# Gate GEMMs of a two-layer recurrence: another spacing, and gates kept on chip

## The chip, the cores and the metric

The kernel runs on one core of one Trainium2 chip. The metric is the device time of one execution in microseconds. The core has five engines that run their own instruction streams and meet at semaphores: TensorE (PE, matmuls into PSUM), VectorE (DVE), ScalarE (ACT), GpSimd (POOL) and SyncE (SP, which here only issues the weight loads).

## The reference

The reference is a two-layer block followed by a second block of one layer, on 16 + 512 tokens of width 1024. What matters here is the mixing part of each of the two layers:

```
c_q, c_kv, k_pe, hq, hf, hi, hg, ga, gb = split_cols(u @ w_in[l], IN_SPLITS)
y_a = mla(...) @ w_proj_attn[l]
y_b = hgrn2(hq, hf, hi, hg, lbs[l], hg_norm[l]) @ w_proj_rec[l]
merged = jax.nn.sigmoid(ga) * y_a + jax.nn.sigmoid(gb) * y_b
h = h + merged @ w_out[l]
```

ga and gb are the gates, 2 x 1024 columns of u @ w_in. hgrn2 is a gated linear recurrence with 4 heads of 128 x 128 state: inside a chunk each output row is a decayed sum over earlier rows, and a state is carried between chunks. Its output is normalised per head, multiplied by silu(hg) and projected.

## The kernel before

Activations lie transposed: 128 channels on the partitions, the tokens along the free dimension (528 in layer 0, the 512 real ones in layer 1's gates and projections). A GEMM unit is one 128-column block of a weight. To keep float32 accuracy each operand is split into a high and a low part, and a unit is three terms (L571 to L576, matmuls at L573 and L575). For each unit SP loads raw weights into one of four slots (L405), ACT makes the high part `wh` (`hi`, L973) and POOL the low part `wl` (`split`, L474). ACT does that for unit k + 3 in `ahead(l, k)`, so the place of that call in ACT's order sets when POOL's split runs. A unit's result goes to one of two PSUM pairs; TensorE may start unit k when VectorE has evacuated unit k - 2 (L562). `evac` (L1396 to L1399) is that evacuation, with a multiplication by `rstd` or by a gate.

The recurrence of a layer goes over five tiles of tokens, of 16 rows and 4 x 128 rows. A tile of 128 rows has 8 levels m = 0 to 7 (the 16-row tile has 5), so there are 37 levels, numbered `lv` = 0 to 36. Level m adds the pairs of rows whose distance falls in blocks of 2^m. For each level VectorE prepares operands `qd` and `kd` (L1704, L1705), updates the running products `suf` and `HF` (L1711, L1713), and merges the result of the level before under a mask (`merge`, L1682 and L1686). TensorE runs four small matmuls per level (L789, shown as x8), may not start level lv before `kd_ready` of it, nor before `merged_lv` of level lv - 2. VectorE's semaphore steps follow one another in order. Behind a tile's last level come `kh` and `qt` (L1717, L1718), four transposes (L801), the output matmuls (L805, L808), the state matmuls (L813) and VectorE's state update (L1723, L1726).

Between the levels TensorE runs the 16 gate GEMMs of the layer (units U_GATE + g, L791 and L792): one behind level 0, and one behind each odd level from 3 to 31. VectorE evacuates a gate into one of two staging buffers `gst` two levels later (`due`, L1660, and `gate`, L1465); ACT applies the sigmoid, stores the gate to `gate_scratch` in memory and runs `ahead` (`gate`, L1051). At the last tile ACT issues the load of all 16 gates to `gat` (`gates_back`, L1063), whose place is that of the activations xh and xl, free by then.

Behind the recurrence (L817 to L836) TensorE sums the squares of two heads (`hg_sum`, L822), then runs the eight projections of the attention branch, two for each head, with the sums of heads 2 and 3 between them, and then the eight of the recurrent branch. Beside it VectorE takes for each head a reciprocal (L1736) and two products (L1737, L1738), waits for `gates_in` once, evacuates two projections with their gates (L1742) and makes a low part (L1744). `merged` (L1477 on VectorE, L1070 on ACT) joins the two branches.

The order on each engine is written out by hand; there is no planner in this part. Parts of the second block use the same gate store and load.

## Time and profile before

| | us |
|---|---|
| median of 3 runs | 3425.16 |
| lowest and highest | 3420.05, 3425.9 |
| the profiled execution | 3419.99 |
| its span, first to last instruction | 3418.1 |
| recurrence of layer 0, first level to last state matmuls | about 672 to 824 |
| recurrence of layer 1 | about 1952 to 2099 |

The profile is of one execution. A row of a timeline gives the start from the span's start, the duration, engine, source line, operation, what it writes and reads, how many such instructions stand together, and in brackets the idle time of the engine just before and who ended it. A matmul in float32 appears as two instructions. PEclk is TensorE's granted clock as a share of the full one; its two levels are 1.2 and 2.4 GHz.

### The profile page before, as it was taken

What the parts mean: (1) busy time and instruction counts of PE and PEld (TensorE: products, weight loads), DVE (VectorE), ACT (ScalarE), POOL (GpSimd) and SP (SyncE); (2) the same over time, 40 slices, a digit from 0 to 9 for tenths busy, and PEclk for the clock granted to TensorE, in tenths of its full rate; (3) what the DMA queues carried; (4) which work ended last, traced back from release to release, by engine and by line L of the source; (5) the groups of instructions that cost most, each with busy time, mean ns of one, the idle gap of its engine ahead of it and who ended that gap; (6) DMA issues with size and microseconds to landing.
All of it is one profiled execution on the core that took longest, in us unless ns stands there. A gap on an engine that the chain in (4) does not pass through costs nothing.

```text
span 3418.1 us, 54419 instructions
## 1 busy us (share of the span) xinstructions
PE 3280.1 (96%) x21472; PEld 2961.2 (87%) x21472; DVE 1392.2 (41%) x2138; ACT 1053.0 (31%) x1485; POOL 1278.9 (37%) x589
## 2 busy tenths in 40 slices
PE   8999989999999999999989998999997988999999
PEld 8999988898999999999989887788775676778887
DVE  4121443477521123121353487522336766552212
ACT  4222433322332224222343322332233433242222
POOL 3444432122444434434432122444436351144443
PEclk9999999999999999999999999999999988999999
DMA  4333321133332323333322133333232432233333
GB/s 131 92 88 91 89 62 50 47 92 106 99 93 87 92 86 93 92 92 89 90 64 62 41 93 111 114 92 96 88 87 65 96 77 91 74 100 98 93 93 98
DMA packets 544842, 298.63 MB, mean 87 GB/s; under 512 B 23281, under 2 KB 528625, under 8 KB 544561
## 3 DMA queue, kind: packets, MB, share of 16 engines
q1 hardware_dynamic: 514128, 258.77, 26.6%
q10 hardware_dynamic: 30560, 37.72, 3.4%
q8 instruction: 108, 1.77, 0.2%
q14 instruction: 46, 0.37, 0.0%
HBM read 278.36 MB, written 16.91 MB: 86 GB/s over the span
## 4 chain that ended last, share of the span: by engine, by line
PE 66%; issue 23%; POOL 6%; DVE 4%; ACT 1%; ACTq 0%; DMA 0%; POOLq 0%; DVEq 0%; SPq 0%
PE pair L575 37%; PE pair L573 27%; POOL wl L474 5%; DVE xl L1413 0%; PE aux L599 0%; DVE negt L1888 0%; DVE tmp L1412 0%; PE aux L930 0%; DVE top L1887 0%; PE aux L931 0%; PE pair L877 0%; ACT xh L987 0%; DVE tmp L1860 0%; PE aux L655 0%; ACT tmp L986 0%
## 5 line engine op out<-in xcount | busy, mean ns | idle before, releaser
L474 POOL TENSOR_TENSOR wl<-raw,wh 128x1024 fp32r<-128x1024 f32 (+4 forms) x549 | 1222.6, 2229 | 2098.8 <-ACT wh L973 2098.3
L973 ACT ACTIVATE wh<-raw 128x1024 fp32r<-128x1024 f32 (+4 forms) x549 | 528.1, 964 | 475.6 <-DMA raw<-ffn_w_down 160.5
L1399 DVE TENSOR_TENSOR tmp<-pair,rstd 128x528 f32<-128x528 f32 (+1 forms) x222 | 155.7, 702 | 812.5 <-PE pair L575 500.1
L575 PE MATMUL pair<-xh,wh 128*128 128x264 f32 x3072 | 462.1, 290 | 17.3 <-DVE xl L1413 12.2
L575 PE MATMUL pair<-xh,wl 128*128 128x264 f32 x3072 | 447.0, 285 | 0.9 <-POOL wl L474 0.9
L575 PE MATMUL pair<-xl,wh 128*128 128x264 f32 x3072 | 447.3, 285 | 0.0
L575 PEld LDWEIGHTS pair<-xh,wh 128*128 128x128 f32 x3072 | 404.4, 190 | 25.3 <-ACT wh L973 9.3
L575 PEld LDWEIGHTS pair<-xh,wl 128*128 128x128 f32 x3072 | 403.4, 189 | 1.2 <-POOL wl L474 1.2
L575 PEld LDWEIGHTS pair<-xl,wh 128*128 128x128 f32 x3072 | 403.9, 189 | 0.0
L1423 DVE SCALAR_TENSOR_TENSOR hT<-pair,hT 128x528 f32 (+3 forms) x144 | 100.7, 700 | 474.0 <-PE pair L575 273.0
L573 PE MATMUL pair<-xh,wh 128*128 128x512 f32 x1064 | 289.5, 405 | 3.7 <-issue 2.2
L573 PE MATMUL pair<-xh,wl 128*128 128x512 f32 x1064 | 282.8, 399 | 5.7 <-POOL wl L474 5.7
L573 PE MATMUL pair<-xl,wh 128*128 128x512 f32 x1064 | 280.1, 396 | 0.0
L573 PEld LDWEIGHTS pair<-xh,wl 128*128 128x128 f32 x1064 | 202.7, 191 | 54.0 <-POOL wl L474 6.5
L573 PEld LDWEIGHTS pair<-xh,wh 128*128 128x128 f32 x1064 | 200.2, 191 | 53.9 <-issue 8.3
L573 PEld LDWEIGHTS pair<-xl,wh 128*128 128x128 f32 x1064 | 201.0, 189 | 45.4
L1013 ACT ACTIVATE ah<-tmp 128x528 f32 (+3 forms) x110 | 70.4, 640 | 533.1 <-DVE tmp L1448 533.1
L575 PE MATMUL pair<-ah,wh 128*128 128x264 f32 x1320 | 203.9, 287 | 13.6 <-DVE R L1630 6.0
L575 PE MATMUL pair<-al,wh 128*128 128x264 f32 x1320 | 201.0, 285 | 0.0
L575 PE MATMUL pair<-ah,wl 128*128 128x264 f32 x1320 | 200.6, 285 | 0.0
L575 PEld LDWEIGHTS pair<-ah,wh 128*128 128x128 f32 x1320 | 177.9, 189 | 16.1 <-issue 11.3
L1010 ACT ACTIVATE tmp<-tmp 128x528 f32<-128x528 f32 (+1 forms) x110 | 70.4, 640 | 353.3 <-DVE tmp L1399 353.3
(320 smaller groups left out, 3973.6 us busy)
## 6 DMA issues: line engine op xcount, KB each, us to landing
raw<-ffn_w_gu SPq DMA_DIRECT2D x176, 512.0 KB, 3.8
raw<-w_in SPq DMA_DIRECT2D x103, 512.0 KB, 3.9
raw<-ffn_w_down SPq DMA_DIRECT2D x64, 512.0 KB, 3.8
raw<-ffn_w_down SPq DMA_DIRECT2D x32, 384.0 KB, 3.3
raw<-w_out SPq DMA_DIRECT2D x24, 512.0 KB, 3.8
raw<-w_ffn_gate SPq DMA_DIRECT2D x22, 512.0 KB, 3.7
raw<-w_ffn_up SPq DMA_DIRECT2D x22, 512.0 KB, 3.8
gate_scratch<-gst ACTq DMA_DIRECT2D x32, 256.0 KB, 2.3
```

The source lines that it names most:

```text
L474: nc.gpsimd.tensor_tensor(wl[:, k % SPL, 0:n], raw[:, k % SPL, 0:n], wh[:, k % SPL, 0:n].bitcast(F32), ALU.subtract).then_inc(S["split_don ...
L573: return nc.tensor.matmul(pp[:, 0, :], wk, x[:, kk, t0:t0 + SEQ], start=first, stop=last)
L575: mm = nc.tensor.matmul(pp[:, h, 0:th], wk, x[:, kk, t0 + h * th:t0 + (h + 1) * th], start=first, stop=last)
L973: nc.scalar.activation(wh[:, k % SPL, 0:n], raw[:, k % SPL, 0:n], ACT.Copy).then_inc(S["split_hi"], 1)
L1010: nc.scalar.activation(tm(SG, T), tm(GS, T), ACT.Silu).then_inc(S["silu_done"], 1)
L1013: nc.scalar.activation(ah[:, bass.ds(j + i * 2, 1), 0:T].rearrange("p o t -> p (o t)"), tm(A32, T), ACT.Copy).then_inc(S["ahi_done"], 1)
L1399: v.tensor_tensor(halves(dst, th), psum_pair(0 if alone else k, th), halves(scale, th), ALU.mult).then_inc(S["evacuated"], 1)
L1423: v.scalar_tensor_tensor(halves(hm, T // 2), psum_pair(k, T // 2), factor, halves(hm, T // 2), ALU.mult, ALU.add).then_inc(S["evacuated"], 1)
```

## The change

Gate GEMMs 0 to 13 stand behind the levels of a list, GATE_AT, which are two or three levels apart: in each tile of 128 rows behind its levels 0, 3 and 6. GEMM 14 stands behind the last tile's state matmuls, GEMM 15 behind the sums of squares of the first two heads. VectorE evacuates gates 0 to 12 two levels later as before, gate 13 ahead of the last tile's last merge, gate 14 ahead of the first head, gate 15 behind the first head's products. ACT's `ahead` calls move along; the sigmoids of gates 14 and 15 come behind the four heads. Each gate of the layers has a place of its own in SBUF (`homes`), so their store and load go. The second block keeps its store and load, with its own functions. The diff, cut to the layers' part:

```diff
@@ -288,7 +288,8 @@
         relb = [ybuf, z_out]
         negq = [negr[:, 64 * i * (i + 1):64 * (i + 1) * (i + 2)] for i in range(4)]
         negm = [negt[:, 64 * i * (i + 1):64 * (i + 1) * (i + 2)] for i in range(4)]
-        gates1 = gat[:, :].rearrange("p (m t) -> p m t", t=T1)
+        homes = [R[:, 4608 + i * T1:4608 + (i + 1) * T1] for i in range(12)] + [negt[:, 0:T1], negt[:, T1:2 * T1], gst[:, 0, :], gst[:, 1, :]]
+        GATE_AT = (0, 3, 5, 8, 11, 13, 16, 19, 21, 24, 27, 29, 32, 35)
         gates2 = gat[:, 0:2 * KD * SEQ].rearrange("p (m t) -> p m t", t=SEQ)
         hgv = [gst[:, 0, :], gst[:, 1, :], negt[:, 0:T1], negt[:, T1:2 * T1]]
...
@@ -788,8 +789,8 @@
                                 lt, rt, n = kd[m % 2][:, h, 0:sz], qd[m % 2][:, h, 0:sz // 2], sz // 2
                             mm = nc.tensor.matmul(bank[lv % 2][0:sz, h * 128:h * 128 + n], lt, rt, start=True, stop=True)
                         mm.then_inc(S["lv_done"], 1)
-                        if lv == 0 or lv >= 3 and lv % 2 == 1 and lv // 2 < 2 * KD:
-                            gemm(l, U_GATE + lv // 2, KD, (xh, xl), T // 2, t0=t0)
+                        if lv in GATE_AT:
+                            gemm(l, U_GATE + GATE_AT.index(lv), KD, (xh, xl), T // 2, t0=t0)
                         lv += 1
                     if i == 0:
                         pe.wait_ge(S["vt_copied"], l * 10 + 10)
...
@@ -822,9 +823,11 @@
                         mm = nc.tensor.matmul((aux45, aux67)[h % 2][:, x, 0:th], ones, tm(HSQ[h % 2])[:, x * th:(x + 1) * th],
                                               start=True, stop=True)
                     mm.then_inc(S["hgss"], 1)
+                gemm(l, U_GATE + 2 * KD - 2, KD, (xh, xl), T // 2, t0=t0)
                 pe.wait_ge(S["s_ready"], l * 5 + 5)
                 hg_sum(0)
                 hg_sum(1)
+                gemm(l, U_GATE + 2 * KD - 1, KD, (xh, xl), T // 2, t0=t0)
                 for h in range(HG):
                     for x in range(2):
                         gemm(l, U_PROJ + 2 * h + x, 4, (ah[:, 0:4, :], al[:, 0:4, :]), T // 2, t0=t0,
...
@@ -1048,24 +1051,18 @@
                     act.wait_ge(S["evacuated"], U(l, ub + m) + 1 + PAIRS)
                     act.dma_start(out[m * P:(m + 1) * P, :], hT[:, m, N_META:T1]).then_inc(S["stored"], 16)
-            def gate(l, ub, g, T, sets):
-
-                act.wait_ge(S["evacuated"], U(l, ub + g) + 1 + PAIRS)
-                if l is None:
-                    ins = nc.scalar.activation(gst[:, g % 2, 0:T], gst[:, g % 2, 0:T], ACT.Tanh, scale=0.5)
-                else:
-                    ins = nc.scalar.activation(gst[:, g % 2, 0:T], gst[:, g % 2, 0:T], ACT.Sigmoid)
-                ins.then_inc(S["gate_sig"], 1)
-                act.wait_ge(S["gate_sig"], sets * (2 * KD) + g + 1)
-                act.dma_start(gscr[g, :, 0:T], gst[:, g % 2, 0:T]).then_inc(gate_stored[g % 2], 16)
-                ahead(l, ub + g)
-
-            def gates_back(l, ub, T, dst, sets):
-
-                for x in range(2):
-                    act.wait_ge(gate_stored[x], sets * (KD * 16) + KD * 16)
-                act.wait_ge(S["gemm_done"], U(l, ub + 2 * KD) + SPL)
-                act.dma_start(dst, gscr[:, :, 0:T].rearrange("m p t -> p m t")).then_inc(S["gates_in"], 16)
+            def gate(l, g, T):
+
+                act.wait_ge(S["evacuated"], U(l, U_GATE + g) + 1 + PAIRS)
+                nc.scalar.activation(homes[g][:, 0:T], homes[g][:, 0:T], ACT.Sigmoid).then_inc(S["gate_sig"], 1)
+
+            def gate2(g):
+
+                act.wait_ge(S["evacuated"], U(None, U_GATE2 + g) + 1 + PAIRS)
+                nc.scalar.activation(gst[:, g % 2, 0:SEQ], gst[:, g % 2, 0:SEQ], ACT.Tanh, scale=0.5).then_inc(S["gate_sig"], 1)
+                act.wait_ge(S["gate_sig"], DEPTH * (2 * KD) + g + 1)
+                act.dma_start(gscr[g, :, :], gst[:, g % 2, 0:SEQ]).then_inc(gate_stored[g % 2], 16)
+                ahead(None, U_GATE2 + g)
             def merged(l, ub, T, m0):
...
@@ -1162,12 +1159,10 @@
                 lv = g = 0
                 for i, (st, sz) in enumerate(TT1):
                     lv += sz.bit_length()
-                    while g < 2 * KD and 2 * g + 3 < lv:
-                        gate(l, U_GATE, g, T, l)
+                    while g < len(GATE_AT) and (GATE_AT[g] + 2 < lv or i == len(TT1) - 1):
+                        gate(l, g, T)
+                        ahead(l, U_GATE + g)
                         g += 1
-                    if i == len(TT1) - 1:
-                        assert g == 2 * KD
-                        gates_back(l, U_GATE, T, gates2 if T == SEQ else gates1, l)
                     act.wait_ge(S["kht_done"], l * 5 + i + 1)
                     nc.scalar.activation(khT[0:sz, :, :], bank[3][0:sz, :].rearrange("p (h k) -> p h k", h=HG),
                                          ACT.Copy).then_inc(S["kht_copied"], 1)
...
@@ -1189,8 +1184,10 @@
                 hg_square(1)
                 for j in range(4):
                     nc.scalar.activation(ah[:, j, t0:T1], oT[:, j, t0:T1], ACT.Copy).then_inc(S["oth"], 1)
+                ahead(l, U_GATE + 2 * KD - 2)
                 hg_rms(0)
                 hg_rms(1)
+                ahead(l, U_GATE + 2 * KD - 1)
                 for h in range(HG):
                     act.wait_ge(S["yb_in"], l * HG + h + 1)
                     nc.scalar.activation(ah[:, 4 + h, :], tm(A32), ACT.Copy).then_inc(S["ybhi"], 1)
...
@@ -1200,6 +1197,8 @@
                         ahead(l, U_PROJ + 2 * h + x)
                     if h < HG - 2:
                         hg_rms(h + 2)
+                for g in (2 * KD - 2, 2 * KD - 1):
+                    gate(l, g, T)
                 merged(l, U_PROJ + KD, T, l * KD)
                 residual(l, U_WO, nb + 3, lambda m: gcur[:, 2 * KD + m:2 * KD + m + 1], T)
                 if l < DEPTH - 1:
...
@@ -1485,11 +1472,12 @@
                         dve.wait_ge(S["m_ready"], m0 + m - 1)
                     buf = tm(MB[m % 2], T)
                     if l is None:
-                        evac_tanh(ub + m, buf, gates[:, KD + m, :])
+                        evac_tanh(ub + m, buf, gates[KD + m])
                     else:
-                        evac(l, ub + m, buf, gates[:, KD + m, :], T // 2)
+                        dve.wait_ge(S["gate_sig"], l * (2 * KD) + KD + m + 1)
+                        evac(l, ub + m, buf, gates[KD + m], T // 2)
                     dve.wait_ge(S["evacuated"], U(l, ub + m) + 1 + PAIRS)
-                    v.tensor_tensor(buf, buf, gates[:, m, :], ALU.add).then_inc(S["m_done"], 1)
+                    v.tensor_tensor(buf, buf, gates[m], ALU.add).then_inc(S["m_done"], 1)
                     if m >= 1:
                         lo(m - 1)
                 lo(KD - 1)
...
@@ -1655,12 +1643,15 @@
                 attention(at1[l], oT, hg_inputs, lambda n: hg_evac(n, 0))
                 t0, T = real(l)
-                gates = gates2 if T == SEQ else gates1
+                gates = [x[:, 0:T] for x in homes]
+
+                def gate(g):
+                    evac(l, U_GATE + g, gates[g], rstd[:, t0:T1], T // 2)
                 def due(lv):
-                    if lv >= 3 and lv % 2 == 1 and lv // 2 - 1 < 2 * KD:
-                        gate(l, U_GATE, lv // 2 - 1, T, l, rstd[:, t0:T1])
+                    if lv - 2 in GATE_AT:
+                        gate(GATE_AT.index(lv - 2))
                 lv = 0
                 for i, (st, sz) in enumerate(TT1):
...
@@ -1716,6 +1707,9 @@
                         lv += 1
                     v.tensor_tensor(kh[:, :, 0:sz], HK[:, :, st:st + sz], suf[:, :, 0:sz], ALU.mult)
                     v.tensor_tensor(qt[:, :, 0:sz], HQ[:, :, st:st + sz], HF[:, :, st:st + sz], ALU.mult).then_inc(S["kq_ready"], 1)
+                    if i == len(TT1) - 1:
+                        assert GATE_AT[-1] == lv - 2
+                        gate(len(GATE_AT) - 1)
                     merge(nl - 1, lv - 1)
                     dve.wait_ge(S["ds_done"], l * 5 + i + 1)
                     ds = bank[3].rearrange("p (h v) -> p h v", h=HG)
...
@@ -1730,6 +1724,7 @@
                 for j in range(4):
                     dve.wait_ge(S["oth"], l * 4 + j + 1)
                     v.tensor_tensor(al[:, j, t0:T1], oT[:, j, t0:T1], ah[:, j, t0:T1].bitcast(F32), ALU.subtract).then_inc(S["yo_ready"], 1)
+                gate(2 * KD - 2)
                 for h in range(HG):
                     dve.wait_ge(S["hgrms"], l * HG + h + 1)
                     g = tm(HRMS[h % 2])
...
@@ -1737,9 +1732,10 @@
                     step(v.tensor_tensor(tm(US), HQ[:, h, :], g, ALU.mult))
                     v.scalar_tensor_tensor(tm(A32), tm(US), pcur[:, 13:14], HGT[:, h, :], ALU.mult, ALU.mult).then_inc(S["yb_in"], 1)
                     if h == 0:
-                        dve.wait_ge(S["gates_in"], l * 16 + 16)
+                        gate(2 * KD - 1)
+                        dve.wait_ge(S["gate_sig"], l * (2 * KD) + KD)
                     for x in range(2):
-                        gated(l, U_PROJ + 2 * h + x, 2 * h + x, gates, T)
+                        evac(l, U_PROJ + 2 * h + x, gates[2 * h + x], gates[2 * h + x], T // 2)
                     dve.wait_ge(S["ybhi"], l * HG + h + 1)
                     v.tensor_tensor(al[:, 4 + h, :], tm(A32), ah[:, 4 + h, :].bitcast(F32), ALU.subtract).then_inc(S["yo_ready"], 1)
                 merged(l, U_PROJ + KD, gates, T, l * KD)
```

## Rows read from the trace of the kernel before

**Rows 1.** the page: span, and part 1, busy time and share of each engine
```profile
span 3418.1 us, 54419 instructions
...
PE 3280.1 (96%) x21472; PEld 2961.2 (87%) x21472; DVE 1392.2 (41%) x2138; ACT 1053.0 (31%) x1485; POOL 1278.9 (37%) x589
```

**Rows 2.** windows: stretch; its us, PE, PEld, DVE, ACT, POOL busy, PEclk, DMA share, GB/s
```profile
689.00:809.00 120.00, 118.73 (x986) 117.74 (x985) 97.97 (x165) 27.25 (x35) 32.28 (x14) 0.99 0.29 84
...
809.00:827.00 18.00, 12.94 (x64) 11.79 (x64) 11.48 (x27) 5.07 (x9) 1.43 (x1) 0.72 0.73 269
...
1968.00:2084.00 116.00, 114.27 (x649) 98.25 (x649) 97.69 (x165) 26.80 (x35) 32.45 (x14) 1.00 0.29 86
...
2084.00:2102.00 18.00, 12.59 (x64) 11.56 (x64) 11.04 (x26) 4.67 (x9) 1.41 (x1) 0.72 0.74 264
```

**Rows 3.** timeline of PE, layer 0: start us, us, engine, line, operation [idle before <-releaser]
```profile
759.35 2.18 PE L575 MATMUL pair<-xh,wh 128*128 128x264 f32 x16
...
765.24 1.00 PE L789 MATMUL aux<-tmp 128*128 128x64 f32 x8
...
766.55 1.10 PE L789 MATMUL aux<-tmp 128*128 128x64 f32 x8 [0.31 <-DVE tmp L1705]
```

**Rows 4.** timeline of DVE, one tile of layer 0, then two state updates of layer 1
```profile
758.74 1.12 DVE L1726 SCALAR_TENSOR_TENSOR R<-R,HF,aux 128x128 f32<-128x128 f32 x4 [3.04 <-PE aux L813]
...
774.12 0.71 DVE L1399 TENSOR_TENSOR gst<-pair,rstd 128x528 f32<-128x528 f32 x1
...
776.92 0.42 DVE L1711 TENSOR_TENSOR tmp<-tmp,HF 128x256 f32<-128x256 f32 x1
...
777.38 2.50 DVE L1713 TENSOR_TENSOR HF<-HF 128x256 f32<-128x256 f32 x1
...
789.70 0.44 DVE L1686 COPY_PREDICATED R<-con,aux 128x256 f32<-128x256 int32 x1 [0.91 <-PE aux L789]
...
793.18 1.12 DVE L1726 SCALAR_TENSOR_TENSOR R<-R,HF,aux 128x128 f32<-128x128 f32 x4 [3.04 <-PE aux L813]
...
2035.16 1.12 DVE L1726 SCALAR_TENSOR_TENSOR R<-R,HF,aux 128x128 f32<-128x128 f32 x4 [3.04 <-PE aux L813]
...
2069.05 1.12 DVE L1726 SCALAR_TENSOR_TENSOR R<-R,HF,aux 128x128 f32<-128x128 f32 x4 [3.04 <-PE aux L813]
```

**Rows 5.** timeline of POOL, the same tile of layer 0
```profile
777.04 2.55 POOL L474 TENSOR_TENSOR wl<-raw,wh 128x1024 fp32r<-128x1024 f32 x1 [5.19 <-ACT wh L973]
```

**Rows 6.** timeline of PE, end of the recurrence of layer 0
```profile
811.82 1.97 PE L789 MATMUL aux<-tmp 128*128 128x64 f32 x8 [2.66 <-DVE tmp L1705]
...
824.87 2.05 PE L822 MATMUL aux<-tmp,con 128*128 128x264 f32 x8 [1.22 <-DVE R L1726]
...
834.87 1.54 PE L575 MATMUL pair<-ah,wh 128*128 128x264 f32 x8 [2.13 <-DVE gat L1399]
...
839.41 1.05 PE L822 MATMUL aux<-tmp,con 128*128 128x264 f32 x4
```

**Rows 7.** timeline of PE, end of the recurrence of layer 1
```profile
2085.73 1.10 PE L789 MATMUL aux<-tmp 128*128 128x64 f32 x8 [1.21 <-DVE tmp L1705]
...
2088.86 1.97 PE L789 MATMUL aux<-tmp 128*128 128x64 f32 x8 [2.02 <-DVE tmp L1705]
...
2100.55 2.05 PE L822 MATMUL aux<-tmp,con 128*128 128x264 f32 x8 [1.22 <-DVE R L1726]
...
2110.49 1.16 PE L573 MATMUL pair<-ah,wh 128*128 128x512 f32 x4 [2.31 <-DVE gat L1399]
```

**Rows 8.** timeline of DVE, first heads of layer 0 behind the recurrence
```profile
829.11 3.45 DVE L1736 RECIPROCAL tmp<-tmp 128x528 f32<-128x528 f32 x1 [0.98 <-ACT tmp L1183]
...
835.88 3.45 DVE L1736 RECIPROCAL tmp<-tmp 128x528 f32<-128x528 f32 x1
```

**Rows 9.** timeline of ACT, first merged tile of layer 0
```profile
861.82 0.65 ACT L1074 ACTIVATE mh<-tmp 128x528 fp32r<-128x528 f32 x1 [3.71 <-DVE tmp L1492]
```

**Rows 10.** DMA issues by line: out<-in engine, count, KB each, us to landing
```profile
gat<-gate_scratch ACTq DMA_DIRECT2D x2, 4096.0 KB, 14.6
```

More of the change, by code:

```diff
@@ L1233, in gates @@
                 for g in range(g0, g1):
-                    gate(None, U_GATE2, g, SEQ, DEPTH)
+                    gate2(g)
             def square2(j):
@@ L1463, in ffn @@
                     f0 += nf
-            def gate(l, ub, g, T, sets, scale):
-                if g >= 2:
-                    dve.wait_ge(gate_stored[g % 2], sets * (KD * 16) + g // 2 * 16)
-                evac(l, ub + g, gst[:, g % 2, 0:T], scale, T // 2)
-            def gated(l, k, m, gates, T):
-                if l is None:
-                    return evac_tanh(k, gates[:, m, :], gates[:, m, :])
-                evac(l, k, gates[:, m, :], gates[:, m, :], T // 2)
             def merged(l, ub, gates, T, m0):
@@ L1866, in gates @@
                 for g in range(g0, g1):
-                    gate(None, U_GATE2, g, SEQ, DEPTH, rstd2[:, :])
+                    if g >= 2:
+                        dve.wait_ge(gate_stored[g % 2], g // 2 * 16)
+                    evac(None, U_GATE2 + g, gst[:, g % 2, 0:SEQ], rstd2[:, :], th)
             def index_score(n):
@@ L1972, in more2 @@
                         if k == U_PROJ2:
-                            dve.wait_ge(S["gates_in"], DEPTH * 16 + 16)
-                        gated(None, k, k - U_PROJ2, gates2, SEQ)
+                            dve.wait_ge(S["gates_in"], 16)
+                        evac_tanh(k, gates2[:, k - U_PROJ2, :], gates2[:, k - U_PROJ2, :])
             def s5_out(n):
@@ L2005, in _ @@
                 v.tensor_tensor(al[:, j, 0:SEQ], oT[:, j, 0:SEQ], ah[:, j, 0:SEQ].bitcast(F32), ALU.subtract).then_inc(S["yo_ready"], 1)
-            merged(None, U_PROJ2 + KD, gates2, SEQ, DEPTH * KD)
+            merged(None, U_PROJ2 + KD, [gates2[:, m, :] for m in range(2 * KD)], SEQ, DEPTH * KD)
             residual(None, U_WO2, 0.5, X2, n2 + 1, lambda m: vec[:, V_GAIN + 64 + m:V_GAIN + 65 + m], SEQ)
```

6 lines of the change are left out of this document (3 added, 3 removed).

## Prediction, made before the change was run

> **What bounds the kernel now.** The page comes first: TensorE is busy for 96% of the span, VectorE for 41% [rows 1]. Over the whole kernel TensorE is the bound, and whatever is only moved from one place on TensorE to another keeps its price. The change touches the recurrence of two layers, so the stages are read next. In the long stretch of the recurrence, before the last levels, TensorE is busy for 118.73 of 120 us, but VectorE for 97.97 of them as well; in the 18 us after it TensorE is busy for 12.94 us only, at a granted clock of 0.72; layer 1 shows the same, 114.27 of 116 us and then a clock of 0.72 [rows 2]. So there are two places with different limits. In the tail (levels 32 to 36, the last state update, the first projections) TensorE waits and runs at the lower of its two clock levels for part of the time: this is what the change fills. In the body TensorE looks full, and the question is how much room VectorE has once GEMMs are taken out of it.
>
> The timeline answers that. TensorE in the body runs a gate GEMM of 5.89 us (759.35 to 765.24), then a level, waits 0.31 us, and runs a second level ahead of the next GEMM [rows 3]. VectorE's state updates stand 34.44 us apart in layer 0 (758.74 to 793.18) and 33.89 us in layer 1 (2035.16 to 2069.05) [rows 4]. Inside that tile VectorE is idle for only two stretches of note: 0.91 us for the last level, and 3.04 us for the matmuls of output and state, which no placement of gate GEMMs removes [rows 4]. The rest is a chain of small steps, one of which takes 2.50 us where the one ahead of it took 0.42 us: it starts 0.34 us after a GpSimd split that lasts 2.55 us (777.04) and ends 0.29 us after it [rows 4, 5]. Each gate GEMM brings one such split with it, so each costs VectorE about 2.08 us beside the evacuation of 0.71 us, some 0.1 of which overlaps the next step and leaves 0.62 [rows 4]. The Trainium skill, "SBUF — State Buffer", section "SBUF: two separate sides", says that VectorE with two SBUF inputs and GpSimd share a port pair under an exclusive lock held for a whole instruction; by that rule the split delays VectorE wherever in the tile it falls. The row agrees with 2.08 us.
>
> **The change part by part.**
>
> *Body.* A full tile (8 levels) now has three gate GEMMs, behind its levels 0, 3 and 6, where it had four. TensorE's work falls from 34.44 to 34.44 - 5.89 = 28.6 us. VectorE's falls by one evacuation, one lock and the idle 0.91 us: 34.44 - 0.62 - 2.08 - 0.91 = 30.8 us. So VectorE's chain becomes the bound of the tile, and TensorE waits about 2 to 3 us in it, in two wide gaps: it has two levels to run behind a GEMM and must wait for the third, whose operands VectorE can only finish after the evacuation and two rounds of steps. These waits run in a ring, since VectorE must in turn wait for the end of a GEMM that started late: stepping through a tile with the spacings of [rows 3, 4], VectorE comes to the evacuation of the second gate at 17.0 us, and that GEMM ends at 17.5 us. I add 0.6 us: 31.4 us. The bounds are 30.8 (no wait) and 33.5 us (a lock of 2.08 us falls ahead of the third level and passes through TensorE in full). The last tile took 30.5 us before (793.14 to 824.87 - 1.22) [rows 4, 6] with its last gates' splits of half size; it now has three GEMMs with full ones, so it is like the others. The 16-row tile loses about 1 us, as its gate is evacuated a level sooner. Layer 0: before 3 x 34.44 + 30.5 = 133.8, after 4 x 31.4 + 1 = 126.6, a gain of 7.2 us. Layer 1: before 3 x 33.89 + 30.3 (2069.05 to 2100.55 - 1.22) = 132.0 [rows 4, 7], after, with the same sum from 33.89, 4 x 31.1 + 1 = 125.4, a gain of 6.6 us.
>
> *The stage behind the last state update.* Before, the first reciprocal of VectorE starts at 829.11 and the second at 835.88, that is 5.5 and 12.2 us after the last state matmuls (823.65), and each later head takes 6.77 us again [rows 6, 8]. A head's TensorE work (two projections of 2.9 us, half of a gate GEMM, and a sum of 0.8 us) is as long, 6.7 us. So this stage has no room either: both engines are full in it. Now TensorE runs gate GEMM 14 (5.9), the two sums (1.7), GEMM 15 (5.9), projection 0 (2.9) and projection 1 (2.9) in a row, and the second head's reciprocal stands on VectorE's queue behind the evacuation of projection 1: 19.3 us plus 1.4 for handing over, that evacuation and one step, some 20.7 us instead of 12.2. Cost 8.5 us in layer 0 and, with 512 columns for 528, 8.2 in layer 1. What waits behind the moved evacuations is ScalarE's next square and the third sum. The two sigmoids of ScalarE come after the heads, where it was idle for 3.71 us before the first merged tile [rows 9]: nothing; without that cover two sigmoids and a table change, some 2.6 us.
>
> *Memory.* The stores of the layers' 32 gates and their two loads of 4 MB (14.6 us to landing) [rows 10] go. In the long stretches the 16 DMA engines were 0.29 busy [rows 2], and no idle time of TensorE ended on a DMA in the rows of the tail [rows 6, 7]: nothing, at most 0.4 us per gate on ScalarE, which is not on the path.
>
> *Sum without the clock:* layer 0 -7.2 + 8.5 = +1.3, layer 1 -6.6 + 8.2 = +1.6, together +3 us. The tail's waits of 2.66, 1.21, 2.02, 1.22, 2.13 and 2.31 us [rows 6, 7] are really filled; they come back as waits in the wide gaps.
>
> *The clock.* Where TensorE had only short levels and a wait between them, it fell: behind the 2.66 us wait the levels take 1.97 us each instead of 1.10 [rows 3, 6], in layer 1 the same after waits of 1.21 and 2.02 us [rows 7]. Behind a wait of 2.13 us the projection takes 4.54 us instead of 2.9 (834.87 to 839.41), and behind 2.31 us in layer 1 the first third takes 1.16 us, so there it did not fall [rows 6, 7]. That is three of four, and a short fall costs 1.6 to 1.8 us. Each layer now has eight wide gaps, each with three short levels and a wait of 1.1 to 2.7 us between two GEMMs. I let 5 or 6 of 8 fall: 5.5 x 1.75 = 9.6 us a layer, 19 us in all, and they count in full, since VectorE waits for the slowed GEMM. Bounds: 0 (none) and 28 us (all).
>
> By the Trainium skill, "TensorE: Matmul & The Clock Gate", section "Why this matters for your kernels", only long idle gaps between bursts make the clock drop, and gaps like these would not. The rows show drops at shorter waits. By that rule the sum stays at +3 us; it is the first rival.
>
> Sum: +3 + 19 = +22 us on the profiled execution of 3419.99 us (span 3418.1 [rows 1] and 1.9 around it), 3442 us. The median of the runs stands 5.2 us above that execution: 3447 us.
>
> **The rivals.**
>
> *A, the clock holds.* The wide gaps are broken by too short waits, and a GEMM stands close on both sides. For it: after 2.31 us it held once. Against: three of four fell, with the same short levels. Time: 3425.2 + 3 = 3428, with the tile bounds 3423 to 3440.
>
> *B, faster.* The tail's gain stays and the body doesn't pay. Mechanism: a lock costs VectorE nothing if it falls into one of its own waits, above all the 3.04 us before the state update; ScalarE no longer spends 0.4 us on issuing the store, so each split starts sooner, and gaps between splits are wider. If one of the three locks of a tile falls into a wait, a tile takes 31.4 - 2.1 = 29.3 us; over eight tiles 17 us, and the clock then holds as the third level comes earlier: 3425.2 + 3 - 17 = 3411 us. It decides from about one hidden lock in every second tile on. Against it: a split follows the evacuation of its gate by 2.9 us (774.12 to 777.04) [rows 4, 5], and no evacuation stands that far ahead of the state matmuls.
>
> *C, the ring is worse.* Locks ahead of the third level in half of the tiles (another 8 us) and nearly all gaps fall (9 us more): 3464 us.
>
> **How the numbers follow.** Forecast (slower by 9 to 33 us) 0.53; A 0.22; B 0.13; C 0.12. Some 0.2%, 7 us, is what a measurement of this kernel can tell from no change. Faster by more: B, and the low end of A, 0.14. Within: most of A, 0.20. Slower: the forecast, C and the top of A, 0.66. The range leaves out B's better half and the upper end of C: 3417 to 3464.
>
> **What would show it.** Right: state updates 31 to 33 us apart; TensorE waiting 1 to 3 us for VectorE behind two levels in tiles 1 to 4; a granted clock of 0.85 to 0.95 in the body where it was 0.99; no wait over 1 us between level 35 and projection 0; the second reciprocal some 20 us behind the last state matmuls. Wrong: tiles under 30.5 us, or a body at full clock (rival A), or locks in the wait for the state matmuls (B). The weakest term is the number of falls.

## The result and the profile after

The changed kernel takes 3488.86 us in the median (3483.77 to 3492.14), the kernel before 3425.53 us beside it. The ratio is 1.0182, with a 95% interval of 1.016 to 1.0205: it is slower by 63 us, where 22 were forecast, and above the range of 3417 to 3464. The sign was right and the size was not: a lock that the prediction had put at nothing fell on the critical operand, and the clock fell more often and at a higher price than it had taken.

The page of the changed kernel, its span and the busy time and share of each engine, to be held against [rows 1]:

```profile
span 3484.0 us, 54385 instructions
...
PE 3319.3 (95%) x21472; PEld 2994.0 (86%) x21472; DVE 1388.7 (40%) x2138; ACT 1054.8 (30%) x1489; POOL 1276.9 (37%) x589
```

TensorE is busy for 39 us more, though it does the same 21472 instructions: they took longer. VectorE and GpSimd are unchanged. The windows say where (columns as in [rows 2]; the first is the same stretch of layer 0 as there, the second the tail, which now ends some 15 us later, the third the whole run of the four 128-row tiles of layer 1):

```profile
689.00:809.00 120.00, 104.02 (x769) 102.36 (x769) 80.34 (x147) 19.93 (x28) 23.40 (x10) 0.89 0.18 45
824.00:842.00 18.00, 16.57 (x141) 16.20 (x140) 12.39 (x24) 6.73 (x12) 3.85 (x2) 1.00 0.10 30
1997.00:2146.00 149.00, 127.65 (x660) 109.65 (x658) 101.10 (x182) 24.76 (x34) 31.02 (x13) 0.87 0.16 41
```

The body, which had 118.73 us of TensorE work in 120 us at a clock of 0.99 [rows 2], now has 104.02 at 0.89. The tail rose from 12.94 us at 0.72 to 16.57 at 1.00, so the waits and the low clock of the tail did go in layer 0; in layer 1 the same 18 us (2131 to 2149) have 16.59 us at 0.91, where they had 12.59 at 0.72. The tiles of layer 1 ran at 0.87 on average.

From here on a tile is counted from the end of the state matmuls of one tile to the end of those of the next. Before, the four tiles of 128 rows took 35.7, 34.5, 34.4 and 30.5 us in layer 0 and 33.4, 33.8, 33.9 and 30.3 us in layer 1: 135.1 and 131.5 us. After, they take 35.1, 38.5, 39.5 and 35.4, and 35.9, 37.8, 37.7 and 37.6: 148.5 and 149.0 us. The 16-row tile ahead of them, counted from its first level, went from 16.7 to 17.7 and from 15.9 to 16.8 us. Here is one such tile of layer 1, TensorE first:

```profile
2077.24 2.11 PE L790 MATMUL aux<-tmp 128*128 128x64 f32 x16
2083.39 1.97 PE L790 MATMUL aux<-tmp 128*128 128x64 f32 x8 [4.04 <-DVE tmp L1696]
2085.12 3.76 PE L574 MATMUL pair<-xh,wh 128*128 128x512 f32 x8
2088.68 2.40 PE L574 MATMUL pair<-xl,wh 128*128 128x512 f32 x8
...
2095.85 1.56 PE L790 MATMUL aux<-tmp 128*128 128x64 f32 x8 [1.18 <-DVE tmp L1696]
2097.17 3.27 PE L574 MATMUL pair<-xh,wh 128*128 128x512 f32 x8
...
2107.56 1.06 PE L814 MATMUL aux<-R,tmp 128*128 128x128 f32 x8
```

There are two wide gaps. In the first TensorE waits for 4.04 us, and the level behind it takes 1.97 us and the first term of the GEMM 3.76 us, at the lower level of the clock; the whole GEMM takes 7.65 us (2085.12 to 2092.77) instead of 5.66 (2071.58 to 2077.24). In the second it waits for 1.18 us, and behind that the clock falls too: the level takes 1.56 us and the GEMM 6.83 us (2097.17 to 2104.00). VectorE and GpSimd in the same tile:

```profile
2080.41 0.45 DVE L1695 TENSOR_TENSOR tmp<-HQ,HF 128x256 f32<-128x256 f32 x1
2080.78 2.56 DVE L1696 TENSOR_TENSOR tmp<-HK,tmp 128x256 f32<-128x256 f32 x1
2083.37 0.42 DVE L1702 TENSOR_TENSOR tmp<-tmp,HF 128x256 f32<-128x256 f32 x1
...
2093.04 0.69 DVE L1398 TENSOR_TENSOR R<-pair,rstd 128x512 f32<-128x512 f32 x1 [5.13 <-PE pair L574]
```

```profile
2080.61 2.45 POOL L475 TENSOR_TENSOR wl<-raw,wh 128x1024 fp32r<-128x1024 f32 x1 [3.04 <-ACT wh L976]
```

More than half of the 4.04 us comes from the second row. It is `kd` of the third level, the very operand that TensorE waits for: 2.56 us instead of 0.41, that is 2.15 us more, under the split that GpSimd had started 0.17 us earlier. It is so in all eight full tiles of the two layers. The last row shows the ring from the other side: VectorE waits for 5.13 us for the GEMM that started late and ran slowly.

The stage behind the last state matmuls of layer 0, on VectorE (state update, first and second reciprocal), to be held against [rows 8]:

```profile
839.04 1.12 DVE L1720 SCALAR_TENSOR_TENSOR R<-R,HF,aux 128x128 f32<-128x128 f32 x4 [3.04 <-PE aux L814]
...
846.47 3.45 DVE L1731 RECIPROCAL tmp<-tmp 128x528 f32<-128x528 f32 x1 [0.92 <-ACT tmp L1178]
...
859.48 3.45 DVE L1731 RECIPROCAL tmp<-tmp 128x528 f32<-128x528 f32 x1
```

The state matmuls end at 838.99, so the first two reciprocals stand at 7.5 and 20.5 us, where they stood at 5.5 and 12.2 us. The third and fourth follow at 27.2 and 35.3 us, for 21.0 and 27.7 before.

### The profile page after: what moved, and what is told of

Same layout as the page of the kernel before. It is cut to its first block, busy times and chain, and to the rows that moved or that the text cites. A ratio compares the mean times of both kernels' runs of the same rounds, so it can differ in the third digit from the quotient of the medians.

```text
span 3484.0 us, 54385 instructions
## 1 busy us (share of the span) xinstructions
PE 3319.3 (95%) x21472; PEld 2994.0 (86%) x21472; DVE 1388.7 (40%) x2138; ACT 1054.8 (30%) x1489; POOL 1276.9 (37%) x589
## 4 chain that ended last, share of the span: by engine, by line
PE 64%; issue 24%; POOL 6%; DVE 4%; ACT 1%; DMA 1%; ACTq 0%; POOLq 0%; DVEq 0%; SPq 0%
PE pair L576 36%; PE pair L574 26%; POOL wl L475 5%; DVE xl L1412 0%; PE aux L600 0%; DVE negt L1886 0%; PE aux L933 0%; DVE top L1885 0%; PE aux L934 0%; DVE tmp L1411 0%; DMA raw<-ffn_w_gu 0%; PE pair L880 0%; DVE tmp L1856 0%; PE aux L656 0%; DVE tmp L1833 0%
## 5 line engine op out<-in xcount | busy, mean ns | idle before, releaser
L576 PE MATMUL pair<-xh,wh 128*128 128x264 f32 x3072 | 470.1, 293 | 18.8 <-DVE xl L1412 13.6
L576 PEld LDWEIGHTS pair<-xh,wh 128*128 128x128 f32 x3072 | 412.2, 193 | 26.7 <-ACT wh L976 9.3
L574 PE MATMUL pair<-xh,wh 128*128 128x512 f32 x1064 | 300.2, 417 | 1.5 <-DVE xl L1412 1.5
L574 PEld LDWEIGHTS pair<-xh,wh 128*128 128x128 f32 x1064 | 208.2, 198 | 53.9 <-issue 5.8
L576 PEld LDWEIGHTS pair<-al,wh 128*128 128x128 f32 x1320 | 178.7, 191 | 0.0
```

Source lines behind the costliest of these rows:

```text
L574: return nc.tensor.matmul(pp[:, 0, :], wk, x[:, kk, t0:t0 + SEQ], start=first, stop=last)
L576: mm = nc.tensor.matmul(pp[:, h, 0:th], wk, x[:, kk, t0 + h * th:t0 + (h + 1) * th], start=first, stop=last)
```

## The experiments

All tile times are read as above, and all ratios are to the kernel before on the same chip in the same sequence of runs. The kernel before took 3429.30 us there for the first four experiments, 3424.93 for the next four and 3426.57 for the last four.

### The gates on chip, with the old spacing

```diff
-        GATE_AT = (0, 3, 5, 8, 11, 13, 16, 19, 21, 24, 27, 29, 32, 35)
+        GATE_AT = (0, 3, 5, 7, 9, 11, 13, 15, 17, 19, 21, 23, 25, 27, 29, 31)
```

The two GEMMs, evacuations, `ahead` calls and sigmoids behind the recurrence go with it.

> The changed kernel with the gate GEMMs back where they stood before (behind level 0 and each odd level to 31, none behind the state matmuls), gates still kept on chip. Theory L+C (the time comes from the wider spacing, through the lock ahead of the third level and the clock that falls in the wide gaps): near the kernel before, 3425 us, perhaps 1 to 3 us under it as ScalarE no longer issues the stores. Rival M (the gates' new places on chip or the missing load cost the time): 3470 us or more, state updates over 36 us apart.

Measured: 3434.17 us, ratio 1.0017 (1.0005 to 1.0029). The tiles take 35.7, 34.0, 34.0 and 30.7 us in layer 0, and 33.1, 33.4, 33.4 and 29.5 in layer 1: 0.4 us less than before each in the middle ones. So keeping the gates on chip costs nothing in the stages that it touches; the median is dealt with at the end of this section. It does one thing that matters later. The same split of a middle tile in layer 1, first in the kernel before (VectorE's `kd` of the third level and the step behind it, then GpSimd), then in this one:

```profile
2045.49 0.41 DVE L1705 TENSOR_TENSOR tmp<-HK,tmp 128x256 f32<-128x256 f32 x1
2045.93 2.58 DVE L1711 TENSOR_TENSOR tmp<-tmp,HF 128x256 f32<-128x256 f32 x1
```

```profile
2045.82 2.41 POOL L474 TENSOR_TENSOR wl<-raw,wh 128x1024 fp32r<-128x1024 f32 x1 [3.55 <-ACT wh L973]
```

```profile
2045.47 2.62 DVE L1690 TENSOR_TENSOR tmp<-HK,tmp 128x256 f32<-128x256 f32 x1
```

```profile
2045.28 2.52 POOL L475 TENSOR_TENSOR wl<-raw,wh 128x1024 fp32r<-128x1024 f32 x1 [3.04 <-ACT wh L974]
```

Before, the split started 0.33 us after `kd` had, and held up the step behind it. Without the store that ScalarE used to issue between sigmoid and `ahead` it starts 0.52 us sooner against `kd`, 0.19 us ahead of it, and `kd` itself takes 2.62 us. At this spacing that is free, since a GEMM stands between the second and the third level. With the new spacing nothing does. There the split starts 2.38 us behind the evacuation of its gate (2078.23 to 2080.61), as in this kernel (2042.90 to 2045.28), where it was 2.90 us with the store (2042.92 to 2045.82). That the store at the new spacing would have kept `kd` free is worked out from these rows: no run has both.

### No lock: the low weight part of the gates written as zeros

```diff
+                nc.gpsimd.memset(wl[:, k % SPL, :].bitcast(F32), 0.0).then_inc(S["split_done"], 1)
```

in place of the split for gate GEMMs 3 to 15; everything else is the changed kernel.

> The changed kernel, but for gate units 3 to 15 GpSimd writes zeros to wl in place of the subtraction raw - wh, so the low part of these weights is left out of the result; the matmuls are the same. In the trace of the changed kernel a split of 2.45 us stood ahead of the third level's operands and stretched that step from 0.41 to 2.56 us. Theory L+C: if zeros hold VectorE up less than the subtraction, each full tile loses 2 us of lock in that gap and 2 to 2.5 us of falls with it, 37.7 us to 33 us, total about 3443 to 3450 us. Clock alone: the step is short but the clock falls all the same, 35.5 us a tile, 3470 us. Rival V (VectorE's own steps are too slow for three levels in a row, lock or not): no change, 3487 us. By the Trainium skill, SBUF - State Buffer, section SBUF: two separate sides, a two-input VectorE step is locked out only by a GpSimd operation that reads SBUF, so zeros should not hold it up at all.

Measured: 3449.35 us, ratio 1.0068 (1.0051 to 1.0084). The tiles take 36.1, 31.3, 31.2, 34.3 and 32.1, 30.4, 32.0, 33.5 us. GpSimd and TensorE in one tile of layer 1 and, for TensorE, the tile behind it:

```profile
2051.11 0.95 POOL L480 MEMSET wl<- 128x1024 f32 x1 [3.75 <-ACT wh L981]
```

```profile
2051.77 1.10 PE L795 MATMUL aux<-tmp 128*128 128x64 f32 x8 [1.40 <-DVE tmp L1701]
2052.69 2.10 PE L579 MATMUL pair<-xh,wh 128*128 128x512 f32 x8
...
2061.41 1.79 PE L795 MATMUL aux<-tmp 128*128 128x64 f32 x8 [1.18 <-DVE tmp L1701]
2062.96 3.05 PE L579 MATMUL pair<-xh,wh 128*128 128x512 f32 x8
...
2083.77 1.10 PE L795 MATMUL aux<-tmp 128*128 128x64 f32 x8 [1.40 <-DVE tmp L1701]
2084.68 3.06 PE L579 MATMUL pair<-xh,wh 128*128 128x512 f32 x8
```

Under these memsets, which read nothing, no step of VectorE in the tiles was held up. The first gap shrinks from 4.04 to 1.40 us; the rest of it is the evacuation and the steps between the GEMM's end and the third level. And the clock: behind a wait of 1.40 us the GEMM's first third ran at full speed in one tile (2.10 us) and at the lower level in the next (3.06 us), and behind 1.18 us it fell. Without locks the kernel is 40 us faster than the changed one, and falls remain in it (clock 0.94 and 0.95 over the four tiles of the layers).

### No falls, as far as fillers go: spare matmuls in the wide gaps

```diff
+        FILL = {7: 20, 10: 8, 15: 20, 18: 8, 23: 20, 26: 8, 31: 20, 34: 8}
...
+                        if lv in FILL:
+                            pe.wait_ge(S["o_evac"], l * 5 + i)
+                        for x in range(FILL.get(lv, 0)):
+                            nc.tensor.matmul(bank[2][:, 0:256], identr[:, :], xh[:, x % 8, 0:256], start=True, stop=True)
```

Added to the changed kernel.

> The changed kernel with extra matmuls of 256 columns into a free PSUM bank behind the second level of each wide gap of the full tiles, 20 in the first gap of a tile and 8 in the second (about 2.2 and 0.9 us, less than the waits of 4.04 and 1.18 us there). They compute nothing that is used. Theory L+C: the clock holds, each full tile goes from 37.7 to 33.3 us (the lock stays), total about 3447 us, granted clock in the body 0.98 or more. If the clock is not a cause but only goes along with the waits: no gain, 3487 us or more.

Measured: 3461.33 us, ratio 1.0102 (1.0083 to 1.012). In layer 0 the clock holds (1.00 over its four tiles) and they take 33.6, 33.9, 33.9 and 33.9 us, 13 us less than in the changed kernel, though TensorE does 112 matmuls more. In layer 1 the 20 fillers, 2.61 us in all, leave a wait of 1.66 us, and one fall stays in each of three tiles (clock 0.96; 34.4, 34.9, 34.9, 33.3 us). The tile was expected at 33.3, some 0.6 us too low, and the total at 3447, 14 us too low. The clock is a cause and not a companion: more work on TensorE made the kernel 28 us faster, 25 of them in the tiles. `kd` still takes 2.58 us here, so these tiles carry the lock without the falls: 33.9 us in layer 0.

### Neither lock nor falls

The zeros of the second experiment, and 8 fillers (1.19 us) in each wide gap.

> Both together: zeros in place of the splits of gate units 3 to 15 (their low weight part is left out of the result), and 8 extra matmuls behind the second level of each wide gap. Theory L+C: no lock and no fall, a full tile takes 30.5 to 31.4 us as I had predicted for the change without falls, total 3423 to 3430 us (what is gained in the body is paid behind it). If the two causes overlap: no better than the better of the two alone, about 3445 us.

Measured: 3438.51 us, ratio 1.0029 (1.0018 to 1.0041). The tiles take 33.0, 31.2, 31.2, 31.2 and 30.6, 30.4, 30.4, 30.4 us, at a clock of 0.99 and 1.00: the tile that was expected (the first of layer 0 apart), although the total is 8 to 15 us above what was. TensorE in one tile of layer 1, fillers and the levels behind them:

```profile
2047.38 1.19 PE L801 MATMUL aux<-xh,identr 128*128 128x256 f32 x8
2048.99 1.10 PE L796 MATMUL aux<-tmp 128*128 128x64 f32 x8 [0.41 <-DVE tmp L1706]
2049.90 2.07 PE L580 MATMUL pair<-xh,wh 128*128 128x512 f32 x8
...
2058.59 1.10 PE L796 MATMUL aux<-tmp 128*128 128x64 f32 x8 [0.18 <-DVE tmp L1706]
```

### Two GEMMs behind the last state update, with the old spacing ahead of them

```diff
-        GATE_AT = (0, 3, 5, 8, 11, 13, 16, 19, 21, 24, 27, 29, 32, 35)
+        GATE_AT = (0, 3, 5, 7, 9, 11, 13, 15, 17, 19, 21, 23, 25, 27)
```

> The first experiment's kernel (gates on chip, GEMMs behind level 0 and each odd level) up to gate GEMM 13 behind level 27; only GEMMs 14 and 15 move behind the last state matmuls, as in the changed kernel. It does the second part of the change alone. My sum for it: tiles 1 to 3 as in the first experiment (34.0 and 33.4 us), the last tile without any GEMM about 26 us instead of 30, the second reciprocal 20.5 us behind the last state matmuls instead of 12.2: +8.3 - 4.5 in each layer, 3434 + 8 = 3442 us, 3438 to 3446. Were the stage behind the recurrence the main cause of the change's loss, it would be at 3470 us or more.

Measured: 3441.05 us, ratio 1.0047 (1.003 to 1.0064), 6.9 us above the first experiment's median. The reciprocals stand at 7.5 and 20.5 us behind the state matmuls in layer 0 and at 7.2 and 19.7 in layer 1, exactly as in the changed kernel. The last tiles fall from 30.7 to 24.75 and from 29.5 to 25.9 us. Two GEMMs of 5.9 us left each of them and only 3.6 to 5.9 us came back: what is left of the tail is VectorE's chain and a clock that was low for much of it (0.65 and 0.60 over the last tiles). The stage costs 8 us a layer wherever the GEMMs came from.

### The same splits, started behind the third level's operand

```diff
+                    if g in (5, 8, 11, 14):
+                        pool.wait_ge(S["kd_ready"], l * LEVELS + GATE_AT[g - 3] + 4)
                     split(l, U_GATE + g, KD)
```

> The changed kernel, but GpSimd holds back one split in each tile of 128 rows (gate units 5, 8, 11, 14) until VectorE has made the third level's operands in the wide gap; nothing is left out. Theory L+C: the lock then falls beside the GEMM that follows, the third level starts 2.1 us sooner and fewer gaps fall: 33 to 34 us a tile instead of 37.7, total 3440 to 3452 us, near the kernel with zeros (3449). If it was not where the lock falls but that there is one: no gain, 3489 us.

Measured: 3456.23 us, ratio 1.0091 (1.0073 to 1.0109). No work is removed, four splits a layer start a little later, and the kernel is 33 us faster than the changed one by the medians, 28 us by the spans of the two profiles, 26.7 of them in the tiles. The tiles take 36.1, 31.7, 34.8, 33.2 and 32.1, 34.3, 34.3, 34.3 us; five of the eight are above the 33 to 34 us that were expected, and the total is 4 us above its range. TensorE in the last tile of layer 1:

```profile
2093.85 1.10 PE L793 MATMUL aux<-tmp 128*128 128x64 f32 x8 [1.89 <-DVE tmp L1699]
2094.76 3.08 PE L577 MATMUL pair<-xh,wh 128*128 128x512 f32 x8
...
2105.06 1.32 PE L793 MATMUL aux<-tmp 128*128 128x64 f32 x8 [1.18 <-DVE tmp L1699]
2106.14 3.50 PE L577 MATMUL pair<-xh,wh 128*128 128x512 f32 x8
```

The first wait is 1.89 us instead of 4.04, and in this tile the clock falls behind both: 3.08 and 3.50 us for a third of a GEMM that takes 2.1 us. In the tile of 31.7 us of layer 0 it fell behind neither.

### Both: splits behind the operand, and 8 fillers a gap

> The kernel that holds back the splits, with 8 extra matmuls of 256 columns behind the second level of each wide gap. Theory L+C: no fall and no lock on the ring, a tile takes 31.3 us in layer 0 and 30.7 in layer 1 as with zeros and extra matmuls, total 3430 to 3440 us, with the whole result computed.

Measured: 3441.96 us, ratio 1.005 (1.0032 to 1.0068), 2 us above what was expected, with every operation of the changed kernel in it. The tiles take 31.4, 31.7, 31.7, 31.7 and 30.7, 31.1, 31.1, 31.1 us at a clock of 1.00: the body that the prediction had drawn. The low weight parts are real ones here, so what the zeros gained was not due to the data. GpSimd's split, the step that it now holds up, and TensorE at that time:

```profile
2048.16 2.63 POOL L476 TENSOR_TENSOR wl<-raw,wh 128x1024 fp32r<-128x1024 f32 x1 [3.70 <-DVE tmp L1704]
```

```profile
2048.12 0.42 DVE L1710 TENSOR_TENSOR tmp<-tmp,HF 128x256 f32<-128x256 f32 x1
2048.58 2.50 DVE L1712 TENSOR_TENSOR HF<-HF 128x256 f32<-128x256 f32 x1
```

```profile
2048.14 1.10 PE L794 MATMUL aux<-tmp 128*128 128x64 f32 x8 [0.90 <-DVE tmp L1704]
...
2057.76 1.10 PE L794 MATMUL aux<-tmp 128*128 128x64 f32 x8 [0.18 <-DVE tmp L1704]
```

The lock of 2.08 us is still there, on the last step of the level (2.50 us for 0.42), and TensorE passes over it with a GEMM.

### Fillers in the tail of the kernel before

```diff
+        FILL = {33: 14, 34: 10, 35: 10}
```

Added to the kernel before, as 128-column matmuls.

> The kernel before with extra matmuls of 128 columns into a free PSUM bank behind levels 33, 34 and 35 (14, 10 and 10), where TensorE waited in the tail and its clock fell to 0.72 of full. If the clock holds, the last tile goes from 30.5 to about 29 us and the output and state matmuls run at full speed: 2 to 4 us less in each layer's tail, total 4 to 8 us under the kernel before. If the tail is VectorE's alone: no gain.

Measured: 3437.75 us, ratio 1.003 (1.001 to 1.0049): a miss. In layer 1 the clock held (1.00 over the four tiles) and the last tile fell from 30.3 to 28.1 us. In layer 0 it rose from 30.5 to 33.5 us:

```profile
807.78 1.76 PE L795 MATMUL aux<-identr 128*128 128x128 f32 x14
810.64 1.97 PE L790 MATMUL aux<-tmp 128*128 128x64 f32 x8 [1.10 <-DVE tmp L1710]
812.37 2.37 PE L795 MATMUL aux<-identr 128*128 128x128 f32 x10
```

Behind 14 fillers and a wait of 1.10 us the level takes 1.97 us, and now the fillers themselves are slow (10 in 2.37 us, where 14 took 1.76) and keep the next level waiting. Here a filler helped where the clock held; where it fell all the same, the filler was paid at the low level. The two tiles together are only 0.8 us longer than before, though the median is 12.8 us up: the rest is not in the stage that was edited (the last section of the experiments).

### Fillers in the tail with the gates on chip

```diff
+        FILL = {33: 8, 34: 6, 35: 6}
```

Added to the first experiment, as 256-column matmuls.

> The gates kept on chip with the old spacing, plus 8, 6 and 6 spare matmuls of 256 columns behind levels 33, 34 and 35 of each layer; their results are used nowhere. If the low clock of the tail is what costs there, the last tile takes 28 to 29 us in both layers (30.7 and 29.5 without them) and the kernel 1 to 4 us less than with the gates on chip alone, 3430 to 3433 us. If the fillers only move the fall of the clock, as in layer 0 of the kernel before with fillers, the last tile of layer 0 takes 33 us and the kernel 3435 to 3438 us.

Measured: 3433.64 us, ratio 1.0019 (1.0004 to 1.0033), and last tiles of 30.4 and 29.8 us for 30.7 and 29.5 without fillers. The clock over the four tiles rises from 0.95 and 0.96 to 0.97 and 0.97, and the fillers' own time takes it back. Neither theory's tile: nothing is won or lost, and no kernel tried here beats the kernel before.

### Three more profiles of the two kernels

The totals of several kernels stood some 10 us above what their tiles say. Their traces, and that of the changed kernel, have a stretch at the lower clock level in the attention of the second block, which the change doesn't touch, and which the first trace of the kernel before doesn't have. The kernel before and the changed one were profiled again, without any edit.

> The kernel before, unchanged, for one more profile. In the second block the trace of the changed kernel has one stretch of 20 to 24 us at the lower clock level, which costs some 10 us and which the first trace of before does not have. Theory S (it comes and goes from execution to execution, whatever the layers do): this profile or the third one of the kernel before shows it, and such an execution takes 3431 to 3438 us where those without it take 3423 to 3427. Theory V (the change brings it): no profile of the kernel before shows it.

> The kernel before, unchanged, once more, for the same question: S expects the low stretch in at least one of the two, at a time of 3431 to 3438 us; V expects none, and times of 3423 to 3427.

> The changed kernel, unchanged, for one more profile. Both theories: tiles of 37.6 to 38.5 us, 3484 to 3492 us. S: the low stretch of the second block can be absent here, and the time is then under 3485 us.

Measured: 3435.62, 3440.90 and 3487.38 us. The same stretch of the second block in the first profile of the kernel before, in the second, in the third, and in the changed kernel (columns as in [rows 2]):

```profile
2916.00:2936.00 20.00, 18.80 (x94) 12.92 (x95) 17.00 (x29) 6.71 (x19) 1.77 (x2) 1.00 0.05 14
```

```profile
2925.00:2945.00 20.00, 20.00 (x56) 13.19 (x56) 11.93 (x20) 4.27 (x12) 0.00 (x0) 0.51 0.00 1
```

```profile
2928.00:2952.00 24.00, 24.00 (x70) 15.82 (x69) 14.09 (x23) 5.00 (x14) 1.27 (x1) 0.51 0.00 1
```

```profile
2974.00:2997.00 23.00, 23.00 (x63) 14.93 (x63) 13.17 (x22) 4.72 (x12) 1.27 (x1) 0.50 0.00 1
```

With this stretch the kernel before ran at 0.51 for 20 to 24 us, and its place behind the stretch is 8 to 10 us later. It belongs to the execution, not to the change. The kernel before with fillers has it too, which is most of its 12.8 us. The 40 other executions of the kernel before in the three sequences lie between 3419.89 and 3437.72 us, 17 of them above 3430; every profile of a kernel with the change or a part of it has the stretch but for one (the zeros without fillers, 3437.63 us where its other executions took 3447.85 to 3452.06). Whether the change makes it more frequent, and by what, is open. Compared like with like, the second and third profiles of before (spans 3433.7 and 3439.0, mean 3436.3) and the two of after (3484.0 and 3485.2, mean 3484.6) lie 48.3 us apart. The other 15 of the 63 us fit this reading but aren't shown one by one: the first profile, from which the forecast counted, doesn't have the stretch, some half of the executions of before take as little time as it or little more, and both profiles of the changed kernel do have it. The second and third profiles of before are also 6 and 11 us behind the first already ahead of the stretch; by what is open. And of the 39 us that TensorE is busy longer in the changed kernel, 17 are there in these two profiles as well (3296.8 and 3297.1 us busy for 3280.1).

## Why the prediction was right in sign and wrong in size

The two layers against the prediction's terms, in us; the third column is read from the runs above.

| term | predicted | measured |
|---|---|---|
| body without locks ahead of the third level, without falls | -7.2 and -6.6 | -7.6 and -6.5 (tiles 126.5 and 124.1 of the kernel with later splits and fillers, for 135.1 and 131.5, and +1.0 and +0.9 in the 16-row tile of the first profile) |
| stage behind the last state update | +8.5 and +8.2 | +8.3 and +7.6 (second reciprocal 20.5 for 12.2, 19.7 for 12.1) |
| a lock ahead of the third level | 0 (a bound) | +8.6 and +8.6 (four tiles x 2.15, as 2.56 - 0.41) |
| falls of the clock | +9.6 and +9.6 | +13.4 and +16.3 (148.5 and 149.0, less 126.5 and 124.1 and less the lock) |
| memory traffic | 0 | 0 in the stages (first experiment) |
| sum | +22 | +48.7, for 48.3 between the profiles that are alike |

The falls can be counted in the changed kernel's own rows. From the start of a gap's third level to the next level behind the GEMM it is 6.8 us in layer 0 and 6.53 in layer 1 where the clock holds; it holds in 3 of the 16 wide gaps, and the other 13 are 1.6 to 3.1 us longer, 13.4 us in layer 0 and 15.0 of the 16.3 in layer 1. Of the 42 us between the forecast of 3447 us and the measured 3488.86, 17 are the lock, some 10 the falls, and some 15 what the last section of the experiments ascribes to the execution.

**The body.** The tile of 31.4 and 31.1 us was right to some 0.3 us (31.7 and 31.1 measured), for the kernel in which nothing locks the third level. Part of that is luck. The prediction took VectorE's chain as the bound and subtracted locks from it; but with all locks gone a tile still takes 31.2 and 30.4 us, only 0.5 and 0.7 less than with three of them, not 6 us less. What bounds it is the round trip in each wide gap: end of a GEMM, evacuation, two rounds of steps, `kd`, level, next GEMM, which leaves TensorE 1.2 to 1.4 us of wait a gap however free VectorE is elsewhere. The prediction did step through this ring, but added only 0.6 us for it to a chain with all its locks (30.8 us), and the chain with locks and the round trip without them happen to be about equally long. Three slips of its working were small: from 33.89 the same sum gives 30.9 us for layer 1 and not 31.1; the first tile of layer 0 took 35.7 us before and not 34.44; and rival A's upper bound, a tile of 33.5 us, gives 3445 us and not 3440.

**The lock, the step that failed.** The prediction named the mechanism and its price (2.08 us, passed through in full, a tile of 33.5 us) and put it at zero, or in rival C in half of the tiles. It fell on `kd` of the third level in every tile, since the order is the same in every tile. The rows to see it were there: the split of [rows 5] starts within a few tenths of a us of the steps it can hold, so 0.5 us decide which one. With the store gone it started 0.52 us sooner against `kd`, and by the rows of the first experiment that is the difference. The prediction mentioned those 0.4 us, but in rival B, as something that gives gaps between splits, and didn't ask onto which instruction the split would move. The experiment that delays four splits a layer is worth 26.7 us in the tiles, 17.2 of them the lock and the rest what the shorter wait does to the clock; the medians are 33 us apart, and the other 6 are not placed.

By the Trainium skill, "SBUF — State Buffer", section "SBUF: two separate sides", a VectorE operation with two SBUF inputs is locked out only by a GpSimd operation that reads SBUF. The runs agree: 2.56 us for 0.41 under a subtraction, and no step of VectorE held under the memset of 0.95 us (tiles 31.2 and 30.4).

**The cover for the sigmoids** held. ScalarE still waits ahead of the first merged tile of layer 0 in the changed kernel, 2.73 us for the 3.71 of [rows 9]:

```profile
886.22 0.65 ACT L1071 ACTIVATE mh<-tmp 128x528 fp32r<-128x528 f32 x1 [2.73 <-DVE tmp L1480]
```

**The falls.** Taken at 5.5 of 8 gaps a layer and 1.75 us each. 13 of 16 fell, where 11 were forecast, and the price was not one price. In the tile shown it is 0.9 + 2.0 us behind the wait of 4.04 us and 0.5 + 1.2 behind that of 1.18; with the splits out of the way it is 1.6 and 1.6 (34.3 less 31.1 us a tile). The tile shown adds up: 31.1, 2.15 for the lock and 4.6 for the two falls give 37.8, and it takes 37.7. But the lock and the clock are not two independent terms. With the longer wait the fall was deeper: 2.15 us of lock cost 3.4 us a tile (37.7 less 34.3, in layer 1).

**The rivals.** A fell: the clock was 0.90 and 0.87, not 0.99. The rule of the Trainium skill on which it leant ("TensorE: Matmul & The Clock Gate", section "Why this matters for your kernels", long idle gaps alone) is not borne out here: it fell behind waits of 1.18 us. B fell: with three gate GEMMs in each tile and the whole result computed no tile came below 30.7 us, and the earlier split was what hurt. Its mechanism was half there: two of the three locks of a tile fell where VectorE had time to spare and cost next to nothing, but TensorE's round trip didn't become shorter by it. C had the right mechanism: with its lock in all tiles instead of half of them it gives 3472 us. It had a chance of 0.12, with a lock that is there in some tiles and not in others, where the rows show the same order in each. Of the signs that the prediction named, three came (no wait over 1 us between level 35 and the projections, the second reciprocal 20 us behind, a clock of 0.85 to 0.95 in the body); the tile of 31 to 33 us didn't, nor did the wait of 1 to 3 us in the first gap of each tile.

**The base.** The forecast was put on an execution of 3419.99 us and lifted by 5.2 us to the median. That median was right (3425.53 us beside the changed kernel). But the execution was one without the low stretch of the second block, and both profiled executions of the changed kernel have it. This is 10 us that no step of the forecast could have known from one profile; the range had to carry it.

## What to carry to other kernels

Here a lock that repeats in every round of a loop fell on the same instruction in every round: before a change shifts an engine by half a microsecond, list which instruction each lock falls on before and after, and treat "ahead of the critical operand" as all or nothing, not as a chance. Work that fills waits in one place opens them in another, and a wait on TensorE between short matmuls can cost more than its length; here waits of 1.2 us cost nothing, or another 1.6 us, or as much as 3.1. If GEMMs are to be spread wider, first move GpSimd's reads behind the operand that TensorE waits for, which cost one wait instruction a tile here and gave back 33 of 63 us by the medians. None of this makes the spread a gain: with the lock moved and the clock held at 1.00 the kernel is still no faster than the kernel before (17 us slower by the medians). The stage behind the last state update costs 8 us a layer, which is what the tiles gain, and the rest isn't in the stages of the change.

## What the runs showed of the hardware that was not expected

- The granted clock fell behind waits of 1.18, 1.20 and 1.40 us between levels, but not each time: behind 1.40 us the next GEMM's first third took 2.10 us in one tile and 3.06 us in the next. The length of the wait alone doesn't decide it.
- Fillers of 1.19 us in each wide gap kept the clock at 1.00 over both layers. Fillers of 1.76 us behind level 33 kept it in layer 1, where no wait followed them, and not in layer 0, where one of 1.10 us did.
- An unchanged program has a stretch of 20 to 24 us in its second block at a clock of 0.51 in some executions and at 1.00 in others, which moves its total by about 10 us. Two further profiles of the kernel before were needed to see that it wasn't the change.
